# A decoder step with a mixture of experts on one core: in one-expert units, gate and up weights become the stationary side of the product

## The chip, the cores and the metric

The kernel runs on one core of a Trainium2 chip. The metric is the device time of one launch in microseconds (us). The engines are TensorE (PE; its weight loads are shown apart as PEld), VectorE (DVE), ScalarE (ACT), GpSimd (POOL) and SyncE (SP), which here issues most of the DMAs. All arrays are f32.

## The reference, cut to what matters

The layer mixes tokens (a gated DeltaNet and a forgetting attention, side by side), normalises, and then mixes channels with a mixture of experts. Only the last part is touched:

```python
def _moe(h, w_router, router_bias, w_gate, w_up, w_down, ws_gate, ws_up, ws_down):
    x = h.reshape(-1, shp[-1])                    # 544 tokens x 1024
    ...                                           # gates (544 x 64): top 8 of 64 experts per token
    def expert(acc, xs):
        wg, wu, wd, ge = xs                       # 1024x256, 1024x256, 256x1024, gate per token
        y = (jax.nn.silu(x @ wg) * (x @ wu)) @ wd
        return acc + ge[:, None] * y.astype(jnp.float32), None
    routed, _ = lax.scan(expert, zeros, (w_gate, w_up, w_down, gates.T))
    shared = (jax.nn.silu(x @ ws_gate) * (x @ ws_up)) @ ws_down
    return routed + shared
```

There are 512 prompt tokens and 32 sample tokens, 64 experts, 256 feed-forward units in each.

## The kernel before

After routing, the tokens of every expert are in lists, and the experts are ranked by their number of tokens. The routed part runs as 52 **units** (`UNITS`, lines 51 to 71) of up to 128 token rows. 32 units belong to one expert and use all 128 rows; 20 are pairs, with two experts on 64 rows each. The order is a fixed pattern written into the string at line 54: in each block of 13 units come X P W N W W N X P W N W W, where X and W are one-expert units and P and N are pairs. Units 0 and 2 are one-expert units, unit 3 is a pair. Weights stream in with three DMAs per expert (`load_expert`, line 1650) into rings of 5 gate/up and 6 down slots. SyncE issues them and waits for the product that last read the slot (lines 1655 and 1657). In a slot, partition p holds rows 8p to 8p+7 of the gate and up matrices and rows 2p and 2p+1 of the down matrix, so feed-forward unit 2p+k of an expert has to be at partition p, half k, for the down product.

For unit u the work is:

- GpSimd gathers 128 token rows from memory (`gather_rows`, L1727).
- TensorE transposes them, 8 blocks of 128x128 (`xT`, `transpose_rows`, L1737) into banks 0 and 1; ScalarE copies the low half (L2122), VectorE the high half (L2441) into `XT`.
- TensorE forms gate and up together (`gate_up`, L1744): the transposed tokens are the stationary side, the weights move, 512 columns at a time, over 8 blocks of the model dimension. Tokens lie on partitions of the result, gate in columns 0 to 255 and up in 256 to 511 of bank 2 or 3. In a pair each expert has 64 stationary columns, and 16 matmuls run two at a time.
- ScalarE takes the SiLU of the gate half (L2128) into `hid`, VectorE multiplies by the up half in place (L2446, semaphore `a_done`).
- TensorE transposes the hidden rows, 2 blocks (`hiddenT`, L1983), into bank 4. The stationary side is every second column of `hid`, by the rearrangement `(f k)` with k=2. VectorE copies them to `hidT` (L2452, semaphore `at_sb2`).
- TensorE forms the down product (`down_half`, L1752), 4 matmuls of 512 columns into banks 5 and 6; ScalarE (L2134) and VectorE (L2458) copy the two halves to `Yb`, and GpSimd scatters the rows to memory (L1731).

TensorE's order is written by hand (lines 2000 to 2009): in step u it does `hiddenT(u - 1)`, `xT(u + 1)`, `gate_up_of(u)`, `down_of(u - 1)`, so that the small work of a unit on ScalarE and VectorE lies beside the products of its neighbours. Behind the loop come units for experts with more tokens than planned (`late_units`; none in this data), a wait for all scattered rows, and the weighted sum with the last normalisation.

Of the kernel before, what the change touches and what calls it, by code (L numbers as in the profile page):

```python
# [7 lines left out]
ALU = mybir.AluOpType  # L8
# [4 lines left out]
P = 128  # L13
D = 1024
KD = D // P
# [13 lines left out]
FF = 256  # L29
# [10 lines left out]
           f=7 * W + 2 * H, ga=7 * W + 3 * H, gb=7 * W + 3 * H + D)  # L40
# [10 lines left out]
UNITS, LOADS = [], []  # L51
for blk in range(4):
    wide, paired = iter(range(6)), iter(range(3))
    for kind in "XPWNWWNXPWNWW":
        n = len(LOADS)
# [10 lines left out]
        else:  # L66
            i = 4 * next(paired) + blk
# [27 lines left out]
def build(nc, A, O):  # L95
    Tick.live.clear()
    sb = nc.alloc_sbuf_tensor("arena", [P, 53200], F32)
    bank = [nc.alloc_psum_tensor(f"bank{i}", [P, 512], F32) for i in range(8)]

    def at(off, *dims, p=P, dt=None):  # L100

        size = int(np.prod(dims))
        v = sb[0:p, off:off + size]
        if dt is not None:
            v = v.bitcast(dt)
        if len(dims) > 1:
            names = "abcde"[:len(dims)]
            v = v.rearrange(f"p ({' '.join(names)}) -> p {' '.join(names)}",
                            **{n: d for n, d in zip(names, dims)})
        return v  # L110
# [921 lines left out]
    u = at(T2 + 6912, W)  # L1032
# [23 lines left out]
    for quarter in range(4):  # L1056
        g = [("gate", quarter, i // 4, i // 2 % 2, i % 2) for i in range(16)]
        a, b = [("raw", 2 * quarter + i) for i in range(2)], [("rows", 2 * quarter + i) for i in range(2)]
# [585 lines left out]
    def gate_up_slot(n):  # L1644
        return at(GU_SLOT[n % RG], 2, KD, FF)
# [20 lines left out]
    def row_indices(step, slots_f, floor_f, to_rows, from_rows):  # L1666
# [12 lines left out]
    XT = [at(X0 + 11520 + D * i, KD, P) for i in range(2)]  # L1679
    Yb = [at(X0 + 13568, D), at(X0 + 14592, D), at(WS0, D), at(WS0 + D, D)]  # L1680
    hid = [at(WS0 + 2 * D + FF * i, FF) for i in range(2)]
    hidT = [at(WS0 + 2 * D + 512 + FF * i, 2, P) for i in range(2)]
# [28 lines left out]
    xt_mm, xt_a, xt_v, gu_mm, silu_d, a_done, at_mm, at_sb2, d_mm, y_a, y_v = (Tick(nc, n) for n in (  # L1711
        "xT_in_psum", "xT_copied_low", "xT_copied_high", "gate_up_product", "silu_done", "hidden_done", "hiddenT_in_psum",
        "hiddenT_copied", "down_product", "y_copied_low", "y_copied_high"))
# [20 lines left out]
    def transpose_rows(half, of):  # L1734
        for k in range(4):
            kk = 4 * half + k
            mm = nc.tensor.transpose(bank[half][:, k * P:(k + 1) * P], of[:, kk * P:(kk + 1) * P], ident)  # L1737
        return mm

    def gate_up(out, x, parts):  # L1740

        for k in range(KD):
            for rows, n in parts:
                mm = nc.tensor.matmul(out[rows].rearrange("p (a n) -> p a n", a=2), x[:, k, rows], gate_up_slot(n)[:, :, k, :],  # L1744
                                      start=k == 0, stop=k == KD - 1)
        return mm

    def down_half(out, half, h, parts):

        for k in range(2):  # L1750
            for rows, n in parts:
                mm = nc.tensor.matmul(out[rows, :], h[:, k, rows], down_slot(n)[:, k, 512 * half:512 * half + 512], start=k == 0, stop=k == 1)  # L1752
        return mm

    def parts_of(loads):
        return [(slice(0, P), loads[0])] if len(loads) == 1 else [(slice(0, 64), loads[0]), (slice(64, P), loads[1])]

    one = [(slice(0, P), 0)]

    def late_units(eng, name, unit):  # L1760

        eng.wait_ge(tab_out.sem, 32)
        n = eng.value_load(count_d, min_val=0, max_val=OVER)
        with eng.If(n > 0):
            with eng.Fori(0, OVER) as i:
                with eng.If(n > i):
                    unit(i)
            eng.sem_inc(after_late[name].sem, 1)
        eng.sem_inc(after_late[name].sem, 1)

    with nc.Block() as block:
        @block.sync
        def _(sp):
# [28 lines left out]
            def late(i):  # L1802
# [3 lines left out]
                load_expert(sp, 0, e, ov_w, ov_w)  # L1806
                sp.dma_start(ov_f, list_rows[bass.ds(row, P), :]).then_inc(ov_l.sem, 16)
            late_units(sp, "sp", late)

            sp.wait_ge(all_rows.sem, 1)  # L1810
# [17 lines left out]
        def _(pe):  # L1828
# [55 lines left out]
            def down(t):  # L1884
                n = TOKS[t]
                pe.wait_ge(s_hid.sem, t + 1)
                if t:
                    pe.wait_ge(sT_sb.sem, t)
                for k in range(2):
                    mm = nc.tensor.transpose(bank[6][:, k * n:(k + 1) * n], shS[t % 2][0:n].rearrange("p (f k) -> p k f", k=2)[:, k, :], ident[0:n, 0:n])  # L1890
                sT_mm.inc(mm)
                pe.wait_ge(sT_sb.sem, t + 1)
                if t:
                    pe.wait_ge(s_fold.sem, t)
                else:
                    pe.wait_ge(h2T_sb.sem, 2 * NT)
                for half in range(2):
                    for k in range(2):
                        mm = nc.tensor.matmul(bank[2 + half][0:n, :], shT[:, k, 0:n], ws[1][:, k, 512 * half:512 * half + 512], start=k == 0, stop=k == 1)  # L1899
                sd_mm.inc(mm)  # L1900
# [57 lines left out]
            unit_rows()  # L1958
            down(4)

            def xT(u):
                pe.wait_ge(g_ld[u % RX].sem, 16 * (u // RX + 1))
                for half, free in enumerate((xt_a, xt_v)):
                    if u:
                        pe.wait_ge(free.sem, u)
                    transpose_rows(half, Xg[u % RX]).then_inc(xt_mm.sem, 1)

            def gate_up_of(u):
                parts = parts_of(UNITS[u][1])
                pe.wait_ge(xt_a.sem, u + 1)  # L1970
                pe.wait_ge(xt_v.sem, u + 1)
                for _, n in parts:
                    pe.wait_ge(gl[n % RG].sem, 32 * (n // RG + 1))
                if u >= 2:
                    pe.wait_ge(a_done.sem, u - 1)
                gate_up(bank[2 + u % 2], XT[u % 2], parts).then_inc(gu_mm.sem, 1)

            def hiddenT(u):
                pe.wait_ge(a_done.sem, u + 1)
                if u:  # L1980
                    pe.wait_ge(at_sb2.sem, u)
                for k in range(2):
                    mm = nc.tensor.transpose(bank[4][:, k * P:(k + 1) * P], hid[u % 2].rearrange("p (f k) -> p k f", k=2)[:, k, :], ident)  # L1983
                mm.then_inc(at_mm.sem, 1)

            def down_of(u):
                parts = parts_of(UNITS[u][1])
                pe.wait_ge(at_sb2.sem, u + 1)
                for _, n in parts:
                    pe.wait_ge(dl[n % RD].sem, 16 * (n // RD + 1))  # L1990
                for half, free in enumerate((y_a, y_v)):
                    if u:
                        pe.wait_ge(free.sem, u)
                    mm = down_half(bank[5 + half], half, hidT[u % 2], parts)
                mm.then_inc(d_mm.sem, 1)
# [17 lines left out]
            def late(i):  # L2013
# [12 lines left out]
                for half in range(2):  # L2026
                    mm = down_half(bank[5 + half], half, hidT[0], one)
                mm.then_inc(ov_d.sem, 1)
            late_units(pe, "pe", late)

            for i, t in enumerate(TAIL):
                n = TOKS[t]
                pe.wait_ge(diag_done.sem, 8 + NPE * i)
                if t == PT:
                    pe.wait_ge(y_ld[t][0].sem, 64)
                    for c in range(2):
                        for half in range(2):
                            mm = nc.tensor.matmul(bank[half][0:n, :], diag[c][:, 0:n], rows_s[:, c, 512 * half:512 * half + 512],  # L2038
                                                  start=c == 0, stop=c == 1)
# [4 lines left out]
                for k in range(NPE):  # L2044
                    if k % 4 == 0:
                        pe.wait_ge(y_ld[t][k // 4].sem, 16)
                    for half in range(2):
                        mm = nc.tensor.matmul(bank[2 * (i % 2) + half][0:n, :], diag[NPE * (i % 2) + k][0:n, 0:n],  # L2048
                                              rows8[t][k // 4][0:n, k % 4, 512 * half:512 * half + 512], start=k == 0, stop=k == NPE - 1)
# [3 lines left out]
        def _(act):  # L2053
# [69 lines left out]

            def silu(u):
                act.wait_ge(gu_mm.sem, u + 1)
                if u >= 2:
                    act.wait_ge(at_mm.sem, u - 1)
                nc.scalar.activation(hid[u % 2], bank[2 + u % 2][:, 0:FF], ACT.Silu).then_inc(silu_d.sem, 1)  # L2128

            def y_low(u):  # L2130
# [110 lines left out]
        def _(dve):  # L2241
# [200 lines left out]

            def hidden(u):
                dve.wait_ge(silu_d.sem, u + 1)
                h = hid[u % 2]
                nc.vector.tensor_tensor(h, h, bank[2 + u % 2][:, FF:2 * FF], ALU.mult).then_inc(a_done.sem, 1)  # L2446

            def hiddenT(u):
                dve.wait_ge(at_mm.sem, u + 1)
                if u >= 2:  # L2450
                    dve.wait_ge(d_mm.sem, u - 1)
                nc.vector.tensor_copy(hidT[u % 2], bank[4][:, 0:2 * P].rearrange("p (k n) -> p k n", k=2)).then_inc(at_sb2.sem, 1)  # L2452
# [46 lines left out]
            for i, t in enumerate(TAIL):  # L2499
                n = TOKS[t]  # L2500
                a, st = acc[i % 2][0:n], st2[i % 2][0:n]
# [4 lines left out]
                for half in range(2):  # L2506
                    cols = slice(512 * half, 512 * half + 512)
# [45 lines left out]
```

## Time and profile before

| | us |
|---|---|
| median of 3 runs | 1933.17 |
| lowest, highest | 1930.46, 1937.65 |
| profiled execution, its own time | 1941.99 |
| its span in the trace | 1940.3 |
| TensorE matmul busy in the span | 1715.4 (88%) |
| VectorE, ScalarE, GpSimd busy | 672.0, 301.8, 321.2 |

The mean granted clock of TensorE over the span is 0.898 of full speed. Times inside the trace count from the span's start. The unit loop lies from about 1240 to 1866 us, a third of the span; the token mixing and the routing come before it, the weighted sum after. A TensorE matmul of f32 data appears as two records, each with a weight load of its own; a transpose appears as one. Matmuls overlap in the pipeline, and their ends are modelled, so the distance between starts says more than a record's length.

### The profile page before, as it was taken

The numbers are of one execution on the slowest core, as the hardware profiler recorded it, in microseconds if no ns is written. First come the engines' busy times: TensorE is split into PE (matmuls) and PEld (weight loads), VectorE is DVE, ScalarE is ACT, GpSimd is POOL, SyncE is SP. The second block draws the span as 40 slices with busy tenths as digits, with TensorE's granted clock in tenths as the row PEclk, the third lists the DMA queues.
The fourth block names the chain that finished last, engine by engine and source line by source line (L and its number), as shares of the span: only waits on it lengthen the run. The fifth ranks groups of instructions, "written<-read, shape, count | busy, mean of one in ns | idle before, by whom it ended". The sixth has DMA issues, their size and how long they took to land. (4 is left out here: it accounts for less than half of the span.)

```text
span 1940.3 us, 19656 instructions
## 1 busy us (share of the span) xinstructions
PE 1715.4 (88%) x7369; PEld 990.1 (51%) x7369; DVE 672.0 (35%) x1279; ACT 301.8 (16%) x636; POOL 321.2 (17%) x338
## 2 busy tenths in 40 slices
PE   5998998779957979999688887879999999999967
PEld 3856553348725767777474443334444444444423
DVE  2002111116548575524454663223111111121118
ACT  1002221102211212222110111001111111111120
POOL 5000000000006995000000032111111111111100
PEclk8995557889978999999798888989999999999989
DMA  9123000202013131421554001699999999989746
GB/s 345 53 87 113 2 1 22 76 15 87 1 47 91 52 105 52 131 100 63 216 183 150 22 14 21 245 389 422 420 399 420 396 356 421 394 362 414 311 183 272
DMA packets 114556, 361.54 MB, mean 186 GB/s; under 512 B 37803, under 2 KB 37931, under 8 KB 88339
## 3 DMA queue, kind: packets, MB, share of 16 engines
q1 hardware_dynamic: 89734, 308.53, 41.3%
q0 software_dynamic: 16112, 35.89, 5.0%
q10 hardware_dynamic: 8614, 15.84, 2.3%
q8 instruction: 60, 0.98, 0.2%
q14 instruction: 36, 0.29, 0.0%
HBM read 336.07 MB, written 43.01 MB: 195 GB/s over the span
## 5 line engine op out<-in xcount | busy, mean ns | idle before, releaser
L1744 PE MATMUL bank<-arena 128*64 128x512 f32 (+1 forms) x1152 | 369.7, 599 | 12.7 <-DMA arena<-in_w_up 12.7
L1744 PEld LDWEIGHTS bank<-arena 128*64 128x64 f32 (+1 forms) x1152 | 139.9, 162 | 205.2 <-issue 205.2
L411 PE MATMUL bank<-arena 128*128 128x272 f32 x896 | 216.9, 405 | 11.1 <-DVE arena L1620 5.1
L411 PEld LDWEIGHTS bank<-arena 128*128 128x128 f32 x896 | 175.3, 197 | 48.9 <-issue 6.2
L419 PE MATMUL bank<-arena 128*128 128x512 f32 (+4 forms) x464 | 174.1, 542 | 26.2 <-ACT arena L2071 15.8
L1752 PE MATMUL bank<-arena 128*64 128x512 f32 (+1 forms) x576 | 190.3, 599 | 0.9 <-DVE arena L2452 0.9
L1092 PE MATMUL bank<-arena 128*128 128x272 f32 x512 | 131.6, 408 | 24.3 <-PEq L966 21.4
L2446 DVE TENSOR_TENSOR arena<-arena,bank 128x256 f32<-128x256 f32 x52 | 21.9, 421 | 345.2 <-ACT arena L2128 345.2
L419 PEld LDWEIGHTS bank<-arena 128*128 128x128 f32 (+1 forms) x464 | 82.2, 211 | 114.0 <-issue 89.0
L1731 POOL DMA_INDIRECT expert_rows<-arena x52 | 52.4, 1007 | 510.5 <-PE bank L1737 456.0
L1752 PEld LDWEIGHTS bank<-arena 128*64 128x64 f32 (+1 forms) x576 | 68.1, 160 | 117.9 <-issue 116.8
L1092 PEld LDWEIGHTS bank<-arena 128*128 128x128 f32 x512 | 96.8, 196 | 49.5 <-issue 24.2
L2458 DVE COPY arena<-bank 128x512 f32<-128x512 f32 x52 | 36.0, 692 | 143.2 <-PE bank L1752 143.2
L2128 ACT ACTIVATE arena<-bank 128x256 f32<-128x256 f32 x52 | 20.0, 384 | 368.3 <-PE bank L1744 368.3
L1252 DVE TENSOR_TENSOR arena<-arena 128x512 f32<-128x512 f32 x48 | 76.5, 1594 | 1.6
L2186 POOL DMA_INDIRECT expert_lists<-arena x34 | 32.9, 967 | 195.6 <-DVE arena L2310 173.1
L1727 POOL DMA_INDIRECT arena<-h_rows,arena x52 | 52.6, 1012 | 51.3 <-DVE arena L1672 33.0
L1176 PE MATMUL bank<-arena 128*128 128x128 f32 x320 | 47.9, 310 | 10.6 <-DVE arena L1287 6.6
L2134 ACT COPY arena<-bank 128x512 f32<-128x512 f32 x52 | 30.5, 587 | 166.7 <-PE bank L1752 166.7
L1737 PE MATMUL bank<-arena 128*128 128x128 f32 x416 | 54.0, 273 | 2.7 <-DMA arena<-h_rows,arena 2.7
L1176 PEld LDWEIGHTS bank<-arena 128*128 128x128 f32 x320 | 44.3, 221 | 17.7 <-issue 17.3
L1400 POOL TENSOR_TENSOR arena<-arena 128x1024 f32<-128x1024 f32 (+5 forms) x48 | 51.8, 1079 | 3.8
(414 smaller groups left out, 1983.4 us busy)
## 6 DMA issues: line engine op xcount, KB each, us to landing
arena<-in_w_gate SPq DMA_DIRECT2D x64, 1024.0 KB
arena<-in_w_up SPq DMA_DIRECT2D x64, 1024.0 KB
arena<-in_w_down SPq DMA_DIRECT2D x64, 1024.0 KB, 17.2
arena<-in_w_ada SPq DMA_DIRECT2D x12, 2048.0 KB, 9.4
arena<-in_w_in SPq DMA_DIRECT2D x11, 2048.0 KB, 7.8
arena<-expert_rows SPq DMA_DIRECT2D x8, 2048.0 KB, 25.3
gate_logits<-arena ACTq DMA_DIRECT2D x16, 272.0 KB, 2.4
arena<-gate_logits SPq DMA_DIRECT2D x8, 544.0 KB, 5.4
```

What stands on the lines that cost most here:

```text
L411: mm = nc.tensor.matmul(pair[i][:, 0:HALF], w[:, k, m * P:(m + 1) * P], rhs[:, k, i * HALF:(i + 1) * HALF], start=k == 0, stop=k == kt - 1)
L419: mm = nc.tensor.matmul(out, lhs[:, k, t * P:t * P + n], w[:, k, cols], start=k == 0, stop=k == kt - 1)
L1092: mm = nc.tensor.matmul(out[:, 0:HALF], w[:, k, m * P:(m + 1) * P], hT[:, k, half * HALF:(half + 1) * HALF], start=k == 0, stop=k == KD - 1)
L1176: mm = nc.tensor.matmul(bank[hb][:, col(h)], Lm[:, h, :], Tm[:, h, :], start=True, stop=True)
L1252: done(lm_done, nc.vector.tensor_tensor(Lm_of[l % 2][:, hs, :], LT[:, hs, :], lvl[:, l, :].unsqueeze(1).to_broadcast([P, 4, P]), ALU.mult))
L1400: step(TT(dst, stmp[:, 0:n, :], stmp[:, n:2 * n, :], ALU.add))
L1727: return nc.gpsimd.indirect_dma_start(out=into, out_offset=None, in_=h2_d, in_offset=bass.IndirectOffsetOnAxis(ap=rows, axis=0), bounds_ch ...
L1731: return nc.gpsimd.indirect_dma_start(out=y_d, out_offset=bass.IndirectOffsetOnAxis(ap=rows, axis=0), in_=of, in_offset=None, bounds_check ...
L1737: mm = nc.tensor.transpose(bank[half][:, k * P:(k + 1) * P], of[:, kk * P:(kk + 1) * P], ident)
L1744: mm = nc.tensor.matmul(out[rows].rearrange("p (a n) -> p a n", a=2), x[:, k, rows], gate_up_slot(n)[:, :, k, :], start=k == 0, stop=k == ...
L1752: mm = nc.tensor.matmul(out[rows, :], h[:, k, rows], down_slot(n)[:, k, 512 * half:512 * half + 512], start=k == 0, stop=k == 1)
L2458: nc.vector.tensor_copy(Yb[u % RY][:, 512:D], bank[6][:, :]).then_inc(y_v.sem, 1)
```

## The change

In one-expert units the roles of the two operands are exchanged: a block of 128 columns of the gate or up weights is stationary, the 128 transposed tokens move. The weight columns are taken with stride 2 (`[:, f, :]` of `(f k)`), so the result has feed-forward units 2p+f of one matrix on partition p. There are 4 such column blocks (gate or up, times even or odd units) with 8 blocks of the model dimension each, 32 matmuls of 128 moving columns instead of 8 of 512. SiLU and product keep their shapes, and VectorE writes the product straight into `hidT`. `hiddenT` is left out for these units on TensorE and VectorE; the semaphores `at_mm` and `at_sb2` count pairs only (`pairs(u)`). Pairs run as before. The late units keep the old form.

```diff
+    def is_pair(u):
+        return len(UNITS[u][1]) == 2
+
+    def pairs(u):
+        return sum(is_pair(i) for i in range(u + 1))
...
+            def wide_gate_up(out, x, n):
+
+                for a in range(2):
+                    for f in range(2):
+                        cols = slice(P * (2 * a + f), P * (2 * a + f) + P)
+                        for k in range(KD):
+                            w = gate_up_slot(n)[:, a, k, :].rearrange("p (f k) -> p k f", k=2)[:, f, :]
+                            mm = nc.tensor.matmul(out[:, cols], w, x[:, k, :], start=k == 0, stop=k == KD - 1)
+                return mm
...
                 if u >= 2:
                     pe.wait_ge(a_done.sem, u - 1)
-                gate_up(bank[2 + u % 2], XT[u % 2], parts).then_inc(gu_mm.sem, 1)
+                if is_pair(u):
+                    gate_up(bank[2 + u % 2], XT[u % 2], parts).then_inc(gu_mm.sem, 1)
+                else:
+                    wide_gate_up(bank[2 + u % 2], XT[u % 2], parts[0][1]).then_inc(gu_mm.sem, 1)
 
             def hiddenT(u):
+                if not is_pair(u):
+                    return
                 pe.wait_ge(a_done.sem, u + 1)
-                if u:
-                    pe.wait_ge(at_sb2.sem, u)
+                if pairs(u - 1):
+                    pe.wait_ge(at_sb2.sem, pairs(u - 1))
...
             def down_of(u):
                 parts = parts_of(UNITS[u][1])
-                pe.wait_ge(at_sb2.sem, u + 1)
+                if is_pair(u):
+                    pe.wait_ge(at_sb2.sem, pairs(u))
+                else:
+                    pe.wait_ge(a_done.sem, u + 1)
...
             def silu(u):
                 act.wait_ge(gu_mm.sem, u + 1)
-                if u >= 2:
-                    act.wait_ge(at_mm.sem, u - 1)
+                if u >= 2 and is_pair(u - 2):
+                    act.wait_ge(at_mm.sem, pairs(u - 2))
+                elif u >= 2:
+                    act.wait_ge(a_done.sem, u - 1)
...
             def hidden(u):
                 dve.wait_ge(silu_d.sem, u + 1)
-                h = hid[u % 2]
-                nc.vector.tensor_tensor(h, h, bank[2 + u % 2][:, FF:2 * FF], ALU.mult).then_inc(a_done.sem, 1)
+                h, up_ = hid[u % 2], bank[2 + u % 2][:, FF:2 * FF]
+                if is_pair(u):
+                    nc.vector.tensor_tensor(h, h, up_, ALU.mult).then_inc(a_done.sem, 1)
+                    return
+                if u >= 2:
+                    dve.wait_ge(d_mm.sem, u - 1)
+                nc.vector.tensor_tensor(hidT[u % 2].rearrange("p k n -> p (k n)"), h, up_, ALU.mult).then_inc(a_done.sem, 1)
 
             def hiddenT(u):
-                dve.wait_ge(at_mm.sem, u + 1)
+                if not is_pair(u):
+                    return
+                dve.wait_ge(at_mm.sem, pairs(u))
```

TensorE's instructions in the middle of the loop, before (a pair's products, then units 4 and 5, both of one expert; L1737 token transposes, L1744 gate and up, L1752 down, L1983 hidden transposes):

```order
L1744 MATMUL bank<-arena 64x512 x16
L1752 MATMUL bank<-arena 128x512 x4
L1983 MATMUL bank<-arena 128x128 x2
L1737 MATMUL bank<-arena 128x128 x8
L1744 MATMUL bank<-arena 128x512 x8
L1752 MATMUL bank<-arena 64x512 x8
L1983 MATMUL bank<-arena 128x128 x2
L1737 MATMUL bank<-arena 128x128 x8
L1744 MATMUL bank<-arena 128x512 x8
L1752 MATMUL bank<-arena 128x512 x4
```

and with the change (L1974 is the matmul in `wide_gate_up`, L2004 the hidden transposes):

```order
L1744 MATMUL bank<-arena 64x512 x16
L1752 MATMUL bank<-arena 128x512 x4
L2004 MATMUL bank<-arena 128x128 x2
L1737 MATMUL bank<-arena 128x128 x8
L1974 MATMUL bank<-arena 128x128 x32
L1752 MATMUL bank<-arena 64x512 x8
L1737 MATMUL bank<-arena 128x128 x8
L1974 MATMUL bank<-arena 128x128 x32
L1752 MATMUL bank<-arena 128x512 x4
```

The 8 wide matmuls of each one-expert unit became 32, and its two hidden transposes are gone; the order is otherwise the same.

The end of the loop on TensorE, before:

```order
L1744 MATMUL bank<-arena 64x512 x16
L1752 MATMUL bank<-arena 128x512 x4
L1983 MATMUL bank<-arena 128x128 x2
L1737 MATMUL bank<-arena 128x128 x8
L1744 MATMUL bank<-arena 128x512 x8
L1752 MATMUL bank<-arena 64x512 x8
L1983 MATMUL bank<-arena 128x128 x2
L1744 MATMUL bank<-arena 128x512 x8
L1752 MATMUL bank<-arena 128x512 x4
L1983 MATMUL bank<-arena 128x128 x2
L1752 MATMUL bank<-arena 128x512 x4
```

and with the change:

```order
L2004 MATMUL bank<-arena 128x128 x2
L1737 MATMUL bank<-arena 128x128 x8
L1974 MATMUL bank<-arena 128x128 x32
L1752 MATMUL bank<-arena 64x512 x8
L1974 MATMUL bank<-arena 128x128 x32
L1752 MATMUL bank<-arena 128x512 x8
```

The down products of the last two units, both of one expert, now follow each other directly.

## Rows read from the trace of the kernel before

**Rows 1.** Windows: busy time of each engine, granted clock, DMA share, GB/s.
```profile
core 0: us, PE busy (x) PEld busy (x) DVE busy (x) ACT busy (x) POOL busy (x), PEclk, DMA share, GB/s
...
1286.90:1866.50 579.60, 577.11 (x2114) 252.97 (x2114) 113.81 (x263) 75.75 (x146) 94.93 (x94) 0.99 0.94 381
...
650.00:700.00 50.00, 47.79 (x382) 37.48 (x380) 18.15 (x22) 9.95 (x19) 47.50 (x31) 1.00 0.28 98
```

**Rows 2.** Waits of SyncE's queue in the unit loop; TensorE's row behind the gap.
```profile
SPq L1659 <- PE bank L1752: 213.7, 36, 11.8
SPq L1659 <- PE bank L1744: 158.7, 25, 18.4
1286.95 3.68 PE L1744 MATMUL bank<-arena 128*64 128x512 f32 x8 [12.74 <-DMA arena<-in_w_up]
```

**Rows 3.** Chain in order of time, 1755 to 1792 us: start, us, what.
```profile
1755.90 0.23 PE bank L1983 x2
1756.13 0.87 PE bank L1737 x8
1757.00 6.87 PE bank L1744 x16
1767.45 0.44 PE bank L1983 x2
...
1775.63 3.43 PE bank L1752 x8
...
1780.17 7.02 PE bank L1744 x32
1787.18 3.63 PE bank L1752 x8
```

**Rows 4.** SiLU, hidden product and hidden copy: ns min/median/max, first and last start.
```profile
L2128 ACT ACTIVATE arena<-bank x52: 384/384/385, 1248.4 to 1856.7; 128x256 f32<-128x256 f32 x52
L2446 DVE TENSOR_TENSOR arena<-arena,bank x52: 420/421/422, 1248.8 to 1857.2; 128x256 f32<-128x256 f32 x52
L2452 DVE COPY arena<-bank x52: 411/414/425, 1249.9 to 1860.8; 128x256 f32<-128x256 f32 x52
```

**Rows 5.** Timeline at the end of the unit loop.
```profile
1857.15 0.42 DVE L2446 TENSOR_TENSOR arena<-arena,bank 128x256 f32<-128x256 f32 x1 [6.69 <-ACT arena L2128]
1859.97 0.39 PE L1983 MATMUL bank<-arena 128*128 128x128 f32 x2
...
1861.24 3.70 PE L1752 MATMUL bank<-arena 128*128 128x512 f32 x8 [0.89 <-DVE arena L2452]
```

**Rows 6.** Timeline of weight loads (PEld) near 661 us and near 138 us.
```profile
661.26 1.86 PEld L1186 LDWEIGHTS bank<-arena 128*128 128x128 f32 x16
663.04 1.45 PEld L1092 LDWEIGHTS bank<-arena 128*128 128x128 f32 x7
138.38 2.31 PEld L419 LDWEIGHTS bank<-arena 128*128 128x128 f32 x20 [0.84 <-issue]
```

**Rows 7.** The two transposes of the loop, by line, and their starts near 1779 us.
```profile
L1983 PEld LDWEIGHTS bank<-arena x104: 194/196/219, 1249.3 to 1860.0; 128*128 128x128 f32 x104
L1983 PE MATMUL bank<-arena x104: 272/283/386, 1249.3 to 1860.1; 128*128 128x128 f32 x104
L1737 PEld LDWEIGHTS bank<-arena x416: 139/141/155, 1238.4 to 1838.6; 128*128 128x128 f32 x139
L1737 PE MATMUL bank<-arena x416: 272/273/301, 1238.5 to 1838.7; 128*128 128x128 f32 x139
1778.90 0.39 PE L1983 MATMUL bank<-arena 128*128 128x128 f32 x2
1779.13 1.04 PE L1737 MATMUL bank<-arena 128*128 128x128 f32 x8
```

**Rows 8.** Timeline: first and last of 16 pairs L1200, L1201.
```profile
664.98 0.33 PE L1200 MATMUL bank<-arena 128*128 128x64 f32 x2
...
670.70 2.10 PE L1092 MATMUL bank<-arena 128*128 128x272 f32 x8
```

## The prediction

> **What bounds the kernel now.** I read the windows first, then the waits, then the order of time on TensorE inside one unit. In the windows [rows 1] the stretch from 1286.9 to 1866.5 us, which holds the unit loop from unit 3 on, has TensorE busy for 577.11 of its 579.60 us at a granted clock of 0.99; the DMA engines are busy for 0.94 of it. Both look full, so the waits decide [rows 2]. TensorE waited once for a weight, 12.74 us, and that wait ends at 1286.95, where this stretch begins. The queue that issues weight loads, on the contrary, waited 213.7 and 158.7 us for TensorE's down and gate/up products to free a slot. So the DMA follows TensorE there, and what TensorE gains or loses in those 580 us is gained or lost in the span.
>
> The chain in order of time [rows 3] is nothing but TensorE. One unit of one expert takes 8 transposes of tokens (L1737, 0.87 us, 0.109 each), the gate/up product (6.87 us, 16 records: each f32 matmul is two passes of 0.429 us with a weight load each), the down product (3.43 to 3.63) and the transposes of the hidden rows (L1983, 0.23 us; 0.44 behind a pair, where 0.21 is the turn from 64-wide to 128-wide stationaries, which then falls on the next transposes and stays). A pair costs 7.02 for gate/up, and the change does not touch it.
>
> **The change, part by part.** 32 of the 52 units hold one expert. Units 0 and 2 run before 1286.95 and what they lose comes out of the 12.74 us wait; if that cover were gone it would cost about 1 us. 30 count.
>
> *Removed.* Per unit the two L1983 transposes, 0.23 us: 30 x 0.23 = 6.9 us, all on the chain. The order of TensorE's instructions confirms that nothing takes their place: L1737 follows the down product directly. VectorE's copy L2452 (0.414 us, [rows 4]) goes too. VectorE is busy for 114 of 580 us, nobody but the last unit waits for it, so this is worth nothing in the loop. At the loop's end it is worth something: down of unit 51 starts at 1861.24 because it waits for L2452, while TensorE had been through with the down product before it at 1859.97, when the last transposes began [rows 5]. Its hidden rows were ready long before (product L2446 from 1857.15, 0.42 us). So 1.27 us go there, 0.23 of them counted already: 1.04 us more.
>
> *Added.* The product's 8 matmuls of 512 moving columns become 32 of 128. The columns streamed stay the same, 16 x 512 before and 64 x 128 now, but the weight loads go from 16 to 64. A load is hidden only while the pass beside it is at least as long. The question of this whole case is therefore the length of a pass with 128 moving columns and a load of 128 columns of its own, read at every second f32 (the slice of `(f k)` with k=2).
>
> The trace has three rows near it [rows 6]. Stream bound: the transposes run at 0.109 us with a contiguous load. Two-pass f32 with a contiguous load: 16 loads of L1186 start at 661.26 and the next line's at 663.04, 1.78 / 16 = 0.111 us. The load alone: L419 with 24 moving columns streams almost nothing and still spans 2.31 us for 20 loads, (2.31 - 0.19) / 19 = 0.112 us. So stream and load are a tie, and anything that slows the load shows.
>
> The stride slows it. L1983 is the one stationary of the loop that is read with this same stride of 2 f32 [rows 7]: its loads take 196 ns against 141 for L1737, and its matmul record has a median of 283 ns, not 273, with the following L1737 as much later: two L1983 passes take 1779.13 - 1778.90 = 0.23 us, not 2 x 0.109 = 0.218. That is 0.010 us per strided load that the stream beside it does not hide. Added to 0.109 or 0.111 it gives 0.119 to 0.121; I take 0.120, since both passes of L1983 have the same two readers on the same memory as the new product (strided stationary, contiguous moving tile).
>
> 64 x 0.120 = 7.68 us in place of 6.87: +0.81 per unit, x 30 = +24.3 us.
>
> *Waits.* The down product of a one-expert unit now waits for the hidden product itself. That comes 0.42 + 0.38 us after the gate/up product [rows 4], and a whole product of 7 us lies between: nothing. VectorE's hidden product gets a wait for the down product of two units ago, which precedes the gate/up product it has just waited for: nothing is held behind it. ScalarE and GpSimd do the same work. A weight slot is freed later by what TensorE loses, so the loads start later and never collide with more than before. TensorE's clock: 128-column passes ran at a granted 1.00 from 650 to 700 us [rows 1], with 382 matmul records in 50 us; the new loop would have about 293 in 50 (2114 + 30 x 46 in some 596 us), so neither clock nor issue is a new limit by that row.
>
> **Sum.** +24.3 - 6.9 - 1.0 = **+16.4 us**. Against the profiled execution, 1941.99 us (its span is 1940.3), 1958.4. The median of the runs shown is 1933.17, 8.8 below the profiled one; the same +16.4 gives **1949.6 us**, +0.85%.
>
> A page speaks against the stride term. The Trainium skill, SBUF — State Buffer, section Door 1 (its note on "cachelines"), says that SBUF has 16-byte lines and that two hits on a line are enough to absorb the latency; a stride of 2 f32 gives just two. By that rule the load costs what a contiguous one does, and the sum would be rival 1's. This trace does not agree: the 283 against 273 ns stands in rows with exactly two hits per line.
>
> **The rivals.**
> *1. Not slower: the stride is free in a long train of loads.* The 0.010 us would be paid once, at the head of two lone loads, not 64 times. For it: only two such loads in a row exist in this trace. Against it: the first one, where it is not prefetched, is late by the same amount. At 0.109 per pass 6.98 us, +0.11 x 30 - 7.9 = -4.6, that is 1928.6; at 0.111 7.10 us, +6.9 - 7.9 = -1.0, that is 1932.2. The sign turns at (6.87 + 7.9 / 30) / 64 = 0.1115 us per pass. No row lets a pass of 128 columns fall under 0.109, so no real gain is in reach.
> *2. Dearer loads.* A two-pass f32 load may pay the stride twice, or suffer beside DMA that is busy 0.94 (0.28 where L1186 was read). At 0.130 us a pass costs 8.32, +1.45 x 30 - 7.9 = +35.6, 1968.8. The far end is the row where loads are not hidden well: L1200 and L1201 alternate stationaries of 128 and 64 columns, two passes each and 16 matmuls in all, and take 670.70 - 664.98 = 5.72 us, 5.72 / 32 = 0.179 us per pass [rows 8]; 11.46 us per unit, +4.59 x 30 - 7.9 = +129.8, 2063.0. I do not take that end, because its passes switch the width and the new ones do not.
> *3. Loads not hidden at all.* Pass = load + stream = 0.112 + 0.109 = 0.221 us, 14.14 per unit, +7.27 x 30 - 7.9 = +210.2, 2143.4. The Trainium skill, TensorE: Matmul & The Clock Gate, Part 3 on packing small matmuls, says that a weight load overlaps a running matmul only where the row groups differ, and here they never do. This trace disagrees: L1186 has both in 0.111 us on full row groups.
>
> **How the numbers follow.** A measurement of this kernel can tell about 0.5%, 9.7 us, from no change. That bound is crossed at (6.87 + (9.7 + 7.9) / 30) / 64 = 0.1165 us per pass. The forecast, a pass of 0.115 to 0.125, spans 1940.0 to 1959.2 and gets 0.65; rival 1 gets 0.17, rival 2 0.15, rival 3 0.03. The range 1930 to 1975 takes in rival 1 nearly whole, the forecast, and rival 2 up to 0.1335 per pass; about 0.15 is left out, most of it above. Slower by over 0.5%: 0.60 of the forecast, rivals 2 and 3, 0.78. Within: 0.05 of the forecast and 0.14 of rival 1, 0.19. Faster: 0.03, for something that no row shows.
>
> **What would show it.** The new product's line should have 2048 matmul records of some 0.28 us, and in the chain each one-expert unit should show it with 7.7 us in place of 6.87, followed by L1737 with no transpose ahead. TensorE should stay busy through the loop, which should end near 1882 in place of 1866.5, with everything behind it shifted alike, and the wait of 12.7 us in unit 3 should shrink by about 1 us. The DMA share should drop a little. 7.0 to 7.1 us would mean rival 1; 8 or more, rival 2, and I would look whether loads or stream are late. If TensorE waits for VectorE or for weights inside the loop, the argument that all is TensorE's own time was wrong.

## The result, and the profile after

Seven runs of each kernel, one beside the other: the changed kernel takes 1945.2 us (1942.39 to 1948.47), the kernel before 1933.17 (1928.19 to 1937.65). The ratio is 1.0061, with a 95% interval from 1.0044 to 1.0079: slower by 11.8 us, between 8.5 and 15.3. The forecast was +16.4 us, a time of 1949.6, in a range from 1930 to 1975.

The spans of the two profiled executions, 1940.3 and 1940.7 us, hide this, because the one of before lost about 10 us ahead of the unit loop: unit 3's product starts at 1286.95 us there and at 1276.61 with the change. The loss is not the change's: runs of other forms of the changed kernel have it, and a run of a form of the kernel before does not (last section). So the loop itself is what to compare, and its end at 1866.8 us says nothing against the 1882 of the prediction, which reckoned with the later start. Windows of the changed kernel, over the loop from unit 3 on and behind it (columns as in rows 1):

```profile
core 0: us, PE busy (x) PEld busy (x) DVE busy (x) ACT busy (x) POOL busy (x), PEclk, DMA share, GB/s
1276.60:1866.80 590.20, 588.09 (x3494) 382.08 (x3494) 103.97 (x233) 74.46 (x146) 94.88 (x94) 1.00 0.93 374
```

The stretch is 590.2 us where it was 579.6 [rows 1]. TensorE is as full as before, its weight loads went from 253 to 382 us busy, VectorE from 114 to 104. The DMA share is 0.93 against 0.94, and SyncE's queue still waits for TensorE, not the other way (waits from 1287 us on, columns as in rows 2):

```profile
SPq L1659 <- PE bank L1752: 222.8, 36, 12.2
SPq L1659 <- PE bank L1744: 124.8, 17, 18.6
SPq L1659 <- PE bank L1974: 27.0, 7, 5.0
```

The chain in order of time, in the part that answers to rows 3 (L1974 is the new product, L2004 a pair's hidden transposes):

```profile
1754.11 0.23 PE bank L2004 x2
1754.34 0.87 PE bank L1737 x8
1755.21 7.54 PE bank L1974 x64
1762.75 3.58 PE bank L1752 x16
1766.33 1.02 PE bank L1737 x8
1767.35 7.54 PE bank L1974 x64
1774.89 3.44 PE bank L1752 x8
1778.33 0.87 PE bank L1737 x8
1779.20 7.02 PE bank L1744 x32
```

A one-expert unit's product takes 7.54 us in 64 passes, 0.1178 each, where it took 6.87 in 16. No transposes of hidden rows stand ahead of L1737. Behind a pair L1737 takes 1.02 us; before, the two kinds of transposes together took 0.44 + 0.87 = 1.31 there, so 0.29 went and not 0.23. By line, the new product (ns min/median/max, first and last start) shows loads that took as long as those of the old strided transposes, 197 against 196 ns [rows 7]:

```profile
L1974 PEld LDWEIGHTS bank<-arena x2048: 194/197/198, 1231.5 to 1857.2; 128*128 128x128 f32 x187
L1974 PE MATMUL bank<-arena x2048: 279/282/385, 1231.6 to 1857.3; 128*128 128x128 f32 x187
```

At the end of the loop the last down product still starts late, now behind ScalarE's copy of the unit before (L2160, the old L2134); this answers to rows 5:

```profile
1857.43 3.60 PE L1752 MATMUL bank<-arena 128*128 128x512 f32 x8
1861.07 0.58 ACT L2160 COPY arena<-bank 128x512 f32<-128x512 f32 x1 [3.05 <-PE bank L1752]
1861.79 3.67 PE L1752 MATMUL bank<-arena 128*128 128x512 f32 x8 [0.77 <-ACT arena L2160]
```

**The account.** I measure the loop from the start of unit 3's product to the start of the last down product and take out unit 3's product, which starts after a wait of over 12 us at the lower clock and varies with it (10.01 and 8.85 us, below; the granted clock is 0.50 to 0.60 in its first 6 us before and in its first 4 us after, then 1.00). Before: 1861.24 - 1286.95 - 10.01 = 564.28 us. After: 1861.79 - 1276.61 - 8.85 = 576.33 us. The difference is +12.05 us, and the terms give the same: 30 x (7.54 - 6.87) = +20.1; transposes 30 x 0.23 = -6.9; 19 of the 30 follow a pair and save 0.06 more, -1.1; the last gap -0.1.

```profile
1286.95 10.01 PE bank L1744 x32
```
```profile
1276.61 8.85 PE bank L1744 x32
```

The first row is of the kernel before, the second of the changed one.

### The profile page after: what moved, and what is told of

Same layout as the page of the kernel before. It is cut to its first block and busy times, and to the rows that moved or that the text cites. A ratio compares the mean times of both kernels' runs of the same rounds, so it can differ in the third digit from the quotient of the medians.

```text
span 1940.7 us, 22536 instructions
## 1 busy us (share of the span) xinstructions
PE 1725.7 (89%) x8841; PEld 1130.3 (58%) x8841; DVE 660.4 (34%) x1247; ACT 299.7 (15%) x636; POOL 320.8 (17%) x338
## 3 DMA queue, kind: packets, MB, share of 16 engines
q1 hardware_dynamic: 89734, 308.53, 41.5%
## 5 line engine op out<-in xcount | busy, mean ns | idle before, releaser
L1974 PE MATMUL bank<-arena 128*128 128x128 f32 x2048 | 246.5, 282 | 0.0
L1974 PEld LDWEIGHTS bank<-arena 128*128 128x128 f32 x2048 | 243.7, 197 | 0.8 <-issue 0.8
L411 PEld LDWEIGHTS bank<-arena 128*128 128x128 f32 x896 | 176.2, 198 | 47.4 <-issue 6.2
L1752 PE MATMUL bank<-arena 128*64 128x512 f32 (+1 forms) x576 | 190.4, 600 | 0.8 <-ACT arena L2160 0.8
L1744 PE MATMUL bank<-arena 128*64 128x512 f32 x640 | 143.5, 602 | 12.5 <-DMA arena<-in_w_up 12.5
L1752 PEld LDWEIGHTS bank<-arena 128*64 128x64 f32 (+1 forms) x576 | 67.3, 160 | 100.3 <-issue 97.9
L1092 PEld LDWEIGHTS bank<-arena 128*128 128x128 f32 x512 | 96.9, 196 | 49.2 <-issue 24.0
L1744 PEld LDWEIGHTS bank<-arena 128*64 128x64 f32 x640 | 44.8, 138 | 97.0 <-issue 97.0
L1737 PEld LDWEIGHTS bank<-arena 128*128 128x128 f32 x416 | 46.5, 141 | 24.6 <-issue 23.2
L1737 PE MATMUL bank<-arena 128*128 128x128 f32 x416 | 55.1, 275 | 2.8 <-DMA arena<-h_rows,arena 2.8
```

Source lines behind the costliest of these rows:

```text
L411: mm = nc.tensor.matmul(pair[i][:, 0:HALF], w[:, k, m * P:(m + 1) * P], rhs[:, k, i * HALF:(i + 1) * HALF], start=k == 0, stop=k == kt - 1)
L1092: mm = nc.tensor.matmul(out[:, 0:HALF], w[:, k, m * P:(m + 1) * P], hT[:, k, half * HALF:(half + 1) * HALF], start=k == 0, stop=k == KD - 1)
L1974: mm = nc.tensor.matmul(out[:, cols], w, x[:, k, :], start=k == 0, stop=k == KD - 1)
```

## Experiments

A pass is one of the two records of an f32 matmul, and stride n means that the stationary block takes every nth f32 of a row. Theory A: the length of a pass is that of its weight load, and the load is slowed by the stride of the stationary side. Its rivals: the train of short two-pass matmuls is slow whatever the stride (B); what was removed was worth nothing (D). The loop time below is always the one just defined. The runs came in two groups, at two times and with the same chip number in the record. Beside the first (the first three subsections) the kernel before took 1943.95 us (23 runs, 1940.78 to 1948.07), beside the second (all others) 1932.88 (23 runs, 1928.83 to 1937.97), so ratios are compared, not times.

### Only the stride taken away

```diff
-                            w = gate_up_slot(n)[:, a, k, :].rearrange("p (f k) -> p k f", k=2)[:, f, :]
+                            w = gate_up_slot(n)[:, a, k, P * f:P * f + P]
```

> The changed kernel with one edit: the stationary block is 128 neighbouring weight columns, not every second one. Hidden units then meet the wrong rows of the down weights, so the output is not the reference's; every instruction, shape, wait and DMA is as in the changed kernel. Changed kernel: a pass every 0.118 us, 7.54 us per one-expert unit. Theory A (the stride of the weight load sets the pass): back to the contiguous two-pass value of L1186, 0.1115 us, 7.14 us per unit, so 30 x 0.40 = 12 us less than the changed kernel, within 2 us of the kernel before. Rival B (it is the train of many short two-pass matmuls, whatever the stride): 7.54 us stays, time as the changed kernel.

Measured: 1945.02 us, ratio to the kernel before 0.9998 (0.9986 to 1.0009); the medians are 1.1 us apart, within that interval. The loop is 1861.75 - 1287.13 - 10.01 = 564.61 us, 11.7 less than in the changed kernel. The chain, and the product by line:

```profile
1757.51 7.15 PE bank L1974 x64
1764.65 3.58 PE bank L1752 x16
1768.24 1.02 PE bank L1737 x8
1769.26 7.15 PE bank L1974 x64
```
```profile
L1974 PEld LDWEIGHTS bank<-arena x2048: 186/192/192, 1241.4 to 1857.2; 128*128 128x128 f32 x187
L1974 PE MATMUL bank<-arena x2048: 275/275/377, 1241.5 to 1857.3; 128*128 128x128 f32 x187
```

7.15 / 64 = 0.1117 us a pass, the 0.1115 of the expectation. B is out. Of the +20.1 us of the new product in the loop, 30 x (7.54 - 7.15) = 11.7 are the stride of 2, and 30 x (7.15 - 6.87) = 8.4 are what the short passes with a load each cost even when the load is contiguous; these 8.4 are paid, but for 0.3 us, by what the transposes and the last gap give back. So the net loss of the changed kernel, +12.05 us in the loop, is the stride. It is all there is to gain, too: with a contiguous load the exchange of sides costs 0.28 us per unit and saves 0.23 to 0.29.

### The same, computing what it should

Two edits beside the one above: the down rows are loaded as `"(k p) n -> p k n"`, so partition p holds rows p and 128+p, and the pairs' hidden transposes read `hid[u % 2][:, k * P:(k + 1) * P]`.

> As the run with contiguous stationary blocks, but computing what the reference wants: the down weights are loaded so that partition p holds rows p and 128+p (two pieces of 4 KB, before one of 8 KB), and the pairs' hidden transposes read neighbouring columns too. Theory A: 7.14 us per unit, 0.22 us for a pair's two transposes, and no price for the pieces since TensorE bounds the loop: 12 to 13 us less than the changed kernel, that is 0 to 2 us off the kernel before. Rival C: the smaller pieces make the weight DMA late, TensorE then shows waits for in_w_down in the loop and the gain is smaller or gone.

Measured: 1943.22 us, ratio 0.9996 (0.9984 to 1.0008). Loop 1866.87 - 1292.46 - 9.95 = 564.46 us. The queue of hardware DMAs moves the same 308.53 MB in 97926 packets instead of 89734, and TensorE waits for no weight from 1300 us to the loop's end. Rival C is out. The pairs' transposes lost their lateness, a median of 273 ns with loads of 141 (283 and 196 in rows 7):

```profile
L2005 PEld LDWEIGHTS bank<-arena x40: 140/141/143, 1265.3 to 1843.3; 128*128 128x128 f32 x40
L2005 PE MATMUL bank<-arena x40: 272/273/273, 1265.7 to 1843.5; 128*128 128x128 f32 x40
```

### Stride 4 and stride 8

```diff
-                            w = gate_up_slot(n)[:, a, k, :].rearrange("p (f k) -> p k f", k=2)[:, f, :]
+                            lo = min((a * KD + k) * FF + f, 2 * KD * FF - 4 * P)
+                            w = at(GU_SLOT[n % RG] + lo, 4 * P).rearrange("p (f k) -> p f k", k=4)[:, 0, :]
```

The diff is written for stride 4; stride 8 has 8 in place of each 4.

> The changed kernel with the stationary block read at every fourth f32 (16 bytes apart), over a span of 512 columns of the same slot; the products are of other numbers, so the output is not the reference's. Theory A: the load gets dearer still. By the lines of 16 bytes (one element on each line) it should be clearly dearer than at stride 2; a linear guess from +0.006 us at stride 2 is +0.013 to +0.02, a pass of 0.125 to 0.13 us, 8.0 to 8.3 us per unit, 14 to 24 us more than the changed kernel. Rival B: no difference.

> The same at every eighth f32 (32 bytes apart); output not the reference's. If what counts is how many elements come from one line of 16 bytes, stride 8 costs the same as stride 4, both having one. If what counts is the distance itself, it costs about twice as much more again (a pass of 0.14 us or longer, 9 us per unit, over 40 us more than the changed kernel).

Measured: 2175.3 and 2189.39 us (one run each), +231 and +245 us on the kernel before. The chain of stride 4, then that of stride 8:

```profile
1749.95 14.47 PE bank L1975 x62
1764.42 3.44 PE bank L1752 x8
```
```profile
1759.29 15.21 PE bank L1975 x64
1774.50 3.44 PE bank L1752 x8
```

14.47 / 62 = 0.233 us a pass at stride 4, 15.21 / 64 = 0.238 at stride 8. For stride 4 my number (0.125 to 0.13) was far off: 0.122 us over the contiguous pass and not 0.013 to 0.02. The cost is not linear in the stride. It doubles where each element is alone on 16 bytes, and hardly grows beyond, as the first alternative of the second expectation has it. These two runs agree with the rule in the Trainium skill, SBUF — State Buffer, section Door 1, that a line of 16 bytes wants two hits: with two the pass is 0.118 us, with one 0.233. Whether a cliff or a slope lies between, only stride 3 (below) can tell.

### Transposes back, wide form kept

```diff
             def hiddenT(u):
-                if not is_pair(u):
-                    return
                 pe.wait_ge(a_done.sem, u + 1)
+                if not is_pair(u):
+                    for k in range(2):
+                        nc.tensor.transpose(bank[7][:, k * P:(k + 1) * P], hidT[u % 2][:, k, :], ident)
+                    return
```

> The changed kernel with one part undone on TensorE: after the hidden product of each one-expert unit, two transposes of 128x128 run again in the old place (into an unused bank, their result is not used; the stationary side is read contiguously). What the removal of the transposes was worth, alone. Theory A: 30 x 0.22 = 6.5 us more than the changed kernel, plus 20 x 0.06 where the unit follows a pair, 7.8 us, some 20 us over the kernel before. Rival D (the transposes stood in the shadow of something and their removal was worth nothing, the rest of the difference coming from the clock or from before the loop): the loop is as long as in the changed kernel.

Measured: 1952.85 us, ratio 1.0106 (1.0088 to 1.0125), against 1.0061 for the changed kernel. Loop 1871.97 - 1279.28 - 10.05 = 582.64 us, +6.3. D is out, A's size was 1.5 us too large. In the chain (L2001 is the transposes put back):

```profile
1775.46 0.37 PE bank L2001 x2
1775.83 0.87 PE bank L1737 x8
1776.70 7.54 PE bank L1974 x64
1784.24 3.44 PE bank L1752 x8
1787.67 0.22 PE bank L2001 x2
1787.89 0.87 PE bank L1737 x8
```

Behind a pair these transposes and L1737 take 0.37 + 0.87 = 1.24 us, not the 1.31 of before, and without them 1.02. So they cost 0.22 each time, 29 x 0.22 = 6.4 in all: in the last unit they fall into the wait for ScalarE's copy, and its down product starts 0.93 us after the one before it ends, as it does without them. The further 0.07 of before belong to the strided load of the first transpose there, which starts together with its matmul (at 1767.38 us in the kernel before) and not 0.42 us ahead of it as elsewhere; here the load is contiguous. The last run on the kernel before (below) tests that by itself.

### Contiguous, and another pair of banks for the last unit

To the edits of the contiguous kernel with matching down rows this adds that the last unit's down product goes to banks 0 and 1 and waits for neither copy:

```diff
+    def y_bank(u, half):
+        return bank[half] if u == NU - 1 else bank[5 + half]
...
-                    if u:
+                    if u and u < NU - 1:
                         pe.wait_ge(free.sem, u)
-                    mm = down_half(bank[5 + half], half, hidT[u % 2], parts)
+                    mm = down_half(y_bank(u, half), half, hidT[u % 2], parts)
```

> The kernel with contiguous stationary blocks and down rows loaded to match (computes what the reference wants), and the last unit's down product goes to banks 0 and 1, so that it waits for no copy of the unit before. Theory A: one-expert unit 7.14 us and no transposes, as measured; the gap ahead of the last down product (0.93 us in the changed kernel) goes, so 1 us under the run without that edit. Against the kernel before: 30 x 0.27 - 30 x 0.23 - 20 x 0.06 - 1.3 = -1.3 us, under what can be measured. Rival E: another wait takes the gap's place (the hidden product, a copy) and the last down product starts as late as before.

Measured: 1932.02 us, ratio 0.9996 (0.9986 to 1.0006). Loop 1849.25 - 1277.20 - 8.52 = 563.53 us, 0.93 less than without the banks. Both down products now stand in one unbroken group of 16 records, and the copies behind them come 3.44 us apart, not 4.43:

```profile
1845.82 7.03 PE L1753 MATMUL bank<-arena 128*128 128x512 f32 x16
1849.45 0.59 ACT L2164 COPY arena<-bank 128x512 f32<-128x512 f32 x1 [3.05 <-PE bank L1753]
1852.89 0.59 ACT L2164 COPY arena<-bank 128x512 f32<-128x512 f32 x1 [2.85 <-PE bank L1753]
```

Rival E is out. The best form of the exchange is thus a draw with the kernel before.

### The kernel before, without its one strided load

The kernel before with the down rows loaded as above and all hidden transposes reading neighbouring columns.

> The kernel before with the down rows loaded as p and 128+p and all hidden transposes reading neighbouring columns: only the stride of L1983's stationary side goes. Theory A: the following matmul is no longer late, each of the 52 pairs of transposes takes 0.218 us instead of 0.229, and the record's median falls from 283 to 273 ns; 0.5 us in the span, which no timing shows. Rival B: 283 ns stays, so the stride was not what made it late.

Measured: 1932.83 us, ratio 0.9997 (0.9986 to 1.0008). The record's median fell to 273 ns, as theory A says, and the loop is 1853.38 - 1280.63 - 10.01 = 562.74 us, 1.5 less than before: my expectation had left out that behind a pair the two transposes fall from 0.44 (rows 3) to 0.37 us. In the total neither can be seen.

```profile
L1984 PEld LDWEIGHTS bank<-arena x104: 138/141/143, 1242.3 to 1852.1; 128*128 128x128 f32 x104
L1984 PE MATMUL bank<-arena x104: 272/273/330, 1242.3 to 1852.2; 128*128 128x128 f32 x104
```
```profile
1759.89 0.37 PE bank L1984 x2
1760.26 0.87 PE bank L1738 x8
```

### Stride 3

As stride 4, with spans of 3 x 128 columns from a start without `+ f`.

> The changed kernel with the stationary block read at every third f32 (12 bytes apart); output not the reference's. Measured so far, per pass: stride 1 0.1115 us, stride 2 0.118, stride 4 0.233, stride 8 0.238. Theory L (a load costs by the lines of 16 bytes that it touches, about 1.82 ns each, and never less than 0.1115): stride 2 touches 64 lines, 0.1165; stride 4 and 8 touch 128, 0.233; stride 3 touches 96, so 0.175 us, 11.2 us per unit, some 110 us over the changed kernel. Rival M (two elements in a row on one line are free, any step to a next line after a single one pays the full price): in stride 3 half of the elements sit alone on their line, and half share one; that gives between 0.175 and the 0.233 of stride 4. Rival N (a cliff between 8 and 16 bytes by distance alone): 0.233 or 0.118.

Measured: 2053.49 us (one run), +121 us. In the chain:

```profile
1759.47 11.10 PE bank L1975 x64
1770.56 3.58 PE bank L1752 x16
1774.14 1.02 PE bank L1737 x8
1775.17 11.09 PE bank L1975 x64
```

11.10 / 64 = 0.1734 us a pass. Theory L asked for 0.175, N for 0.233 or 0.118. All five strides, with the lines of 16 bytes that 128 elements touch:

| stride | lines | us a pass | ns per line |
|---|---|---|---|
| 1 | 32 | 0.1117 | 3.5 |
| 2 | 64 | 0.1178 | 1.84 |
| 3 | 96 | 0.1734 | 1.81 |
| 4 | 128 | 0.2334 | 1.82 |
| 8 | 128 | 0.2377 | 1.86 |

From stride 2 on a load costs about 1.82 ns per line; contiguous loads have another bound of 0.1117. Stride 2 is close to where the two cross. So it is a slope by lines and no cliff. M left the value open between 0.175 and 0.233, and at its lower end, which is L's number, it is not told apart from L. The DMA beside the loads is not what makes them dear: its share between 1300 and 1840 us was 0.96 at stride 2, 0.84 at stride 3 and 0.75 and 0.73 at strides 4 and 8, at the same price per line. Strides 3, 4 and 8 rest on one run each; their effects, over 120 us, are far above the spread of about 10 us between runs.

## Why the prediction was right, and where not

- **TensorE sets the loop, DMA follows: right.** The weight queue waits for TensorE after the change too, TensorE for no weight in the loop, and the loop's +12.05 us stands in the total as +11.8.
- **Clock and issue: right.** The granted clock is 1.00 with 3494 records in 590 us.
- **The stride term: right in kind, too large.** The forecast was 0.120 us a pass, measured 0.1178: +0.67 us per unit instead of +0.81, so 4.2 of the 4.4 us between +16.4 and +12.0; the two misses below, 1.1 and 0.9 us with opposite signs, nearly cancel, which is luck. The failed step is adding L1983's 0.010 us to the pass. The pass is the longer of stream and load; a strided load of 0.118 instead of 0.112 is no more than 0.118, however late it made a lone transpose that could otherwise go at 0.109. The same reading gives 0.009 for the lone transpose; rows 7 showed 0.010.
- **The rule that spoke against the term.** By the rule of the Trainium skill (SBUF — State Buffer, section Door 1) two hits on a line are enough; measured +0.006 us a pass. That is small for one load and all of the result for 1920 of them. The prediction's stride term was right against it. For one hit on a line the rule was right that it is much dearer and my straight line was not; at stride 3 neither had the value.
- **Transposes: right, 1.1 us too small.** -6.9 us expected; put back they cost 6.3 us of loop. The other 1.1 come from 19 places behind pairs. The prediction put all of the 0.21 us there on the turn from 64-wide to 128-wide stationaries, which stays; 0.15 stayed (1.02 - 0.87), and 0.06 went with the strided load that started late.
- **The last gap: wrong by 0.9 us.** The step reckoned with a down product that is free once the hidden rows are ready, and did not ask what is late next: bank 5, which ScalarE still copies out. Of 1.04 us only 0.1 came. Other banks brought the rest.
- **Cover of units 0 and 2: not as forecast.** The wait for the first late weight was 12.52 us, 12.74 before, and should have shrunk by about 1. The prediction reckoned with the longer products, less the two transposes of each unit. In unit 0 TensorE also waited 0.93 us for the hidden product ahead of the transposes, and this wait went with them. From the start of unit 0's product to the start of the long wait it is 32.85 us before and 32.47 with the change: the two units lost nothing. The start of unit 0 and what follows, before and with the change:

```profile
1241.36 7.03 PE L1744 MATMUL bank<-arena 128*128 128x512 f32 x16
1249.33 0.51 PE L1983 MATMUL bank<-arena 128*128 128x128 f32 x2 [0.93 <-DVE arena L2446]
```
```profile
1231.62 7.70 PE L1974 MATMUL bank<-arena 128*128 128x128 f32 x64
1239.16 1.04 PE L1737 MATMUL bank<-arena 128*128 128x128 f32 x8
```

- **Rivals.** 1 (free stride) did not happen; where its sign turns, at a pass of 0.1115, is where the contiguous kernel lies, 0.3 us from before. 2 and 3 did not happen at stride 2: neither a stride paid twice nor the busy DMA showed, and a pass was not the sum of load and stream. The strides of 3 and more show what 2 would have looked like.

## What to carry to other kernels

When the weights become the stationary side, count loads: the stream stays, the loads multiply, and a pass of 128 f32 columns is already as short as its own load (0.109 against 0.112 us), so such an exchange pays only if it removes more than it adds in loads. Lay the stationary operand out contiguously, or at the very least with two elements on each 16 bytes; here the layout was free, because the next product's weights could be loaded in the matching order. When a stall at a loop's end is removed, look at once for the buffer that the previous step still holds.

## What was not expected of the hardware

- A weight load at stride 2 costs 5% more than a contiguous one, at stride 3 55% and at stride 4 109%, with stride 8 barely above stride 4.
- A strided load that starts only with its matmul costs more: the two transposes behind a pair took 0.44 us strided and 0.37 contiguous.
- In the routing ahead of the loop TensorE can lose up to 10 us at one place with no wait that the profile shows. In the changed kernel 64 small matmuls take about 1 us; in the profiled execution of before they came in clumps (timelines, the changed kernel first):

```profile
1171.20 1.14 PE L1866 MATMUL bank<-arena 128*32 128x64 f32 x64 [0.35 <-ACT arena L2095]
```
```profile
1175.05 1.08 PE L1860 MATMUL bank<-arena 128*32 128x64 f32 x32 [5.21 <-issue]
1177.52 0.37 PE L1860 MATMUL bank<-arena 128*32 128x64 f32 x2 [1.39 <-issue]
1178.94 0.26 PE L1860 MATMUL bank<-arena 128*32 128x64 f32 x1 [1.06 <-issue]
```

The four profiles of the first group of runs have these clumps (6 to 9 us from first to last), the four of the second do not (1 us), and the kernel before was 11 us apart between the two groups. The clumps stand in the kernel before and in four forms of the changed kernel, and are absent in the changed kernel, three of its forms and one form of the kernel before, so the change is not their cause; both groups carry the same chip number. Why they come was not tried. They account for the two spans being equal. That they also put the profiled execution of before 8.8 us above its median, and the two groups 11 us apart, fits but is not shown, since no trace of the other executions was kept.
